# Expert loop of a mixture-of-experts block: order of gate/up and down over the items, shape of the weight chunks, place of the down bias

## The reference

```python
top_vals, top_idx = lax.top_k(logits, 4)
top_w = softmax(top_vals)
# for each expert e, over the tokens that chose it:
gu = xb @ w_gate_up[e] + b_gate_up[e]          # (.., 2048)
gate = minimum(gu[:, :1024], 7.0)
up = clip(gu[:, 1024:], -7.0, 7.0)
hid = (up + 1.0) * gate * sigmoid(1.702 * gate)
y = hid @ w_down[e] + b_down[e]                # (.., 1024)
out[token] += y * top_w
```

## Time and profile before

| | us |
|---|---|
| median of 3 runs | 2227.3 |
| lowest, highest | 2226.61, 2228.27 |
| span of the profiled execution | 2221.8 |
| TensorE busy | 2018.8 (91%) |
| DVE busy | 1551.4 (70%) |
| ACT busy | 1263.3 (57%) |
| GpSimd busy | 513.2 (23%) |

### The profile page before, as it was taken

One profiled execution on the slowest core, in us unless ns is written; L12 is line 12 of the kernel. 1 busy time (PEld: TensorE's weight loads), 2 busy tenths in 40 slices (PEclk: granted clock), 3 DMA queues, 4 the chain that ended last, 5 costly groups with the idle time before them and its releaser, 6 DMA issues. The chain is left out here.

```text
span 2221.8 us, 27993 instructions
## 1 busy us (share of the span) xinstructions
PE 2018.8 (91%) x9545; PEld 1620.9 (73%) x9545; DVE 1551.4 (70%) x1320; ACT 1263.3 (57%) x1173; POOL 513.2 (23%) x396
## 2 busy tenths in 40 slices
PE   7999997888799994999999999999999999999990
PEld 6888886777788874777777777777777777777770
DVE  3433565665423346788888888888888888888885
ACT  4223443333333222777777777777777777777771
POOL 2000005555200002123222222322222223223230
PEclk9999998999899995999999999999999999999995
DMA  4232211120023225899999999999999999999965
GB/s 154 84 106 92 98 38 29 29 67 0 27 88 133 95 79 180 300 344 331 353 334 340 350 329 351 334 337 354 331 345 342 328 359 328 345 345 330 356 233 208
DMA packets 227631, 511.33 MB, mean 230 GB/s; under 512 B 18052, under 2 KB 27396, under 8 KB 226500
## 3 DMA queue, kind: packets, MB, share of 16 engines
q1 hardware_dynamic: 218228, 476.65, 61.5%
q0 software_dynamic: 9360, 34.08, 3.9%
HBM read 484.98 MB, written 20.97 MB: 228 GB/s over the span
## 5 line engine op out<-in xcount | busy, mean ns | idle before, releaser
L1736 DVE TENSOR_TENSOR mlo<-mraw,mhi 128x2048 fp32r<-128x2048 f32 x386 | 909.1, 2382 | 169.1 <-ACT mhi L1685 169.1
L1685 ACT ACTIVATE mhi<-mraw 128x2048 fp32r<-128x2048 f32 x386 | 732.5, 1913 | 174.7 <-PE PM L1816 174.3
L1813 PE MATMUL PM<-mhi,xgT_hi 128*128 128x512 f32 x1024 | 414.4, 405 | 0.0
L1814 PE MATMUL PM<-mlo,xgT_hi 128*128 128x512 f32 x1024 | 407.3, 398 | 0.0
L1816 PE MATMUL PM<-mhi,xgT_lo 128*128 128x512 f32 x1024 | 322.3, 396 | 0.0
L1813 PE MATMUL PM<-mhi,hT_hi 128*128 128x512 f32 x512 | 209.1, 408 | 36.3 <-DVE hT_lo L1761 36.3
L1813 PEld LDWEIGHTS PM<-mhi,xgT_hi 128*128 128x128 f32 x1024 | 193.3, 189 | 65.1 <-issue 23.7
L1663 POOL TENSOR_TENSOR glu<-glu 128x512 f32<-128x512 f32 x64 | 146.5, 2290 | 397.4 <-DVE glu L1755 397.4
L1816 PEld LDWEIGHTS PM<-mhi,xgT_lo 128*128 128x128 f32 x1024 | 192.7, 188 | 46.6
L1814 PEld LDWEIGHTS PM<-mlo,xgT_hi 128*128 128x128 f32 x1024 | 193.1, 189 | 43.4
L1814 PE MATMUL PM<-mlo,hT_hi 128*128 128x512 f32 x512 | 202.4, 395 | 0.0
(11 more groups left out here) (309 smaller groups left out, 3025.2 us busy)
## 6 DMA issues: line engine op xcount, KB each, us to landing
mraw<-in_w_gate_up_dram SPq DMA_DIRECT2D x512, 512.0 KB, 5.2
mraw<-in_w_down_dram SPq DMA_DIRECT2D x256, 512.0 KB, 6.9
raw<-in_w_in_dram SPq DMA_DIRECT2D x28, 1024.0 KB, 5.1
qkvT<-in_w_in_dram SPq DMA_DIRECT2D x8, 1024.0 KB, 5.2
mraw<-expert_rows_scratch SPq DMA_DIRECT2D x8, 1024.0 KB, 11.4
stage<-qkvT SPq DMA_DIRECT2D x3, 1536.0 KB, 7.8
qkvT<-in_w_o_gdn_dram SPq DMA_DIRECT2D x4, 1024.0 KB, 5.1
qkvT<-in_w_o_sconv_dram SPq DMA_DIRECT2D x4, 1024.0 KB, 5.0
```

Source lines behind the costliest of these rows:

```text
L1685: nc.scalar.activation(mhi[:, m % SPL], mraw[:, m % RAW], ACT.Copy).then_inc(e_h, 1)
L1736: nc.vector.tensor_tensor(mlo[:, m % SPL], mraw[:, m % RAW], mhi[:, m % SPL].bitcast(F32), ALU.subtract).then_inc(e_l, 1)
L1813: pe.matmul(PM[:, bank + n, :], t_hi[:, k, :], w_hi[:, kk, n, :], start=False, stop=False)
L1814: pe.matmul(PM[:, bank + n, :], t_hi[:, k, :], w_lo[:, kk, n, :], start=False, stop=False)
```

## The change

The 12 chunks of an item stay 1 MB each, but a gate/up chunk is now 128 whole rows of 2048 columns (8 KB runs, one transfer), and a down chunk is two blocks of 128 whole rows (4 KB runs, one transfer). One gate/up pass goes over all four banks with 8 chunks. The loop's body is now: gate/up of item i + 1 with the turning of item i's hidden rows after its third chunk, then down of item i, with the turning of the tokens of item i + 2 after its first chunk. The first gate/up stands ahead of the loop and the last down behind it. Clamps, sigmoid, gating, the GpSimd product, the splits of hidden and tokens and the y copy handle 1024 columns at once. The hidden and the token rows share banks 6 and 7. `expert`, `pick` and `bias` have 128 rows (the added ones are zero) and `pick` has a column per item. The bias of down is no longer added in the loop: routing builds `mix_w` (token x expert mixing weights), and behind the loop TensorE multiplies it with `b_down`; the last block adds that to `h_rows`. GpSimd's share in splitting the bias and chunk 0 goes to DVE.

The core of the diff (the waits and bodies that only change their index are left out):

```diff
-        EARLY = 1
+        FIRST = 8
...
+        def load_gate_up(sp, e, k, m):
+            one = gu[bass.ds(e, 1), k].rearrange("a p c -> (a p) c")
+            sp.dma_start(mraw[:, raw_slot(m), :], one).then_inc(s_mraw[raw_slot(m)], 16)
...
+        def weights_hi(act, i, m):
+            act.wait_ge(s_mraw[raw_slot(m)], 16 * loads_of_slot(i, m))
+            act.wait_ge(e_used, chunk_number(i, m) + 1)
+            nc.scalar.activation(mhi[:, split_slot(m), :], mraw[:, raw_slot(m), :], ACT.Copy).then_inc(e_h, 1)
...
                 for half in range(2):
                     rows = slice(E * half, E * half + E)
-                    sp.dma_start(bias_raw[rows, 0:2 * D], b_gate_up[0]).then_inc(s_br, 16)
-                    sp.dma_start(bias_raw[rows, 2 * D:3 * D], b_down[0]).then_inc(s_br, 16)
-                for m in range(RAW + EARLY):
-
-                    wait(sp, e_l, m - RAW + 1)
-                    load_weights(sp, 0, m)
+                    sp.dma_start(bias_raw[rows, :], b_gate_up[0]).then_inc(s_br, 16)
+                for k in range(RAW):
+                    load_gate_up(sp, 0, k, 4 + k)
+                sp.dma_start(b_out[:], b_down[0]).then_inc(s_br, 16)
...
-                act.wait_ge(s_br, 64)
-                nc.scalar.activation(bias[:], bias_raw[:], ACT.Copy).then_inc(s_bh, 1)
+                act.sem_inc(e_used, SPL)
+                act.wait_ge(s_br, 48)
+                nc.scalar.activation(bias[0:2 * E, :], bias_raw[:], ACT.Copy).then_inc(s_bh, 1)
+                weights_hi(act, -1, 4)
                 act.wait_ge(s_d4, 1)
                 nc.scalar.activation(ex4, d4, ACT.Exp).then_inc(s_ex4, 1)
+                for m in range(5, 8):
+                    weights_hi(act, -1, m)
...
+                link(nc.vector.tensor_tensor(at_place[:], chosen[:], weight[:].unsqueeze(2).to_broadcast([P, K4, E]), ALU.mult))
+                link(nc.vector.tensor_reduce(mix_w[:], at_place[:].rearrange("p (t k) e -> p t e k", t=TT), AX, ALU.add))
+                for m in range(4, 6):
+                    weights_lo(dve, -1, m)
...
+                with pool.Fori(0, last) as i:
+
+                    pool.wait_ge(s_tx, i + 2)
+                    gather(i + 2)
+                    pool.wait_ge(s_th, i + 1)
+                    hidden(i + 1)
+                    scatter(i)
...
+                with act.Fori(0, last) as i:
+                    for m in range(2, 6):
+                        weights_hi(act, i, m)
+                    hidden_hi(i)
+                    for m in range(6, 12):
+                        weights_hi(act, i, m)
+                    sigmoid(i + 1)
+                    tokens_hi(i + 2)
+
+                    act.wait_ge(e_used, chunk_number(i, 0) + 1 + SPL)
+                    pick_expert(i + 2)
+                    weights_hi(act, i, 12)
+                    weights_hi(act, i, 13)
+                    y_copy(i)
...
+                with dve.Fori(0, last) as i:
+                    for m in range(2, 6):
+                        weights_lo(dve, i, m)
+                    hidden_lo(i)
+                    for m in range(6, 11):
+                        weights_lo(dve, i, m)
+                    clamp(i + 1)
+                    weights_lo(dve, i, 11)
+                    gated(i + 1)
+                    tokens_lo(i + 2)
+                    weights_lo(dve, i, 12)
+                    weights_lo(dve, i, 13)
...
+                with pe.Fori(0, last) as i:
+
+                    pe.wait_ge(s_gate, i + 1)
+                    pe.wait_ge(s_up, i + 1)
+                    gate_up(i + 1, 0)
+                    down(i, 8, between=i + 2)
+                pe.wait_ge(s_gl, last + 2)
+                turn_hidden(last)
+                down(last, 0)
...
                 for t in range(TT):
+                    dve.wait_ge(s_bo, 2 * t + 2)
+                    nc.vector.tensor_tensor(h_rows[:, t, :].rearrange("p (b c) -> p b c", b=2), PM[:, 2 * t:2 * t + 2, :],
+                                            h_rows[:, t, :].rearrange("p (b c) -> p b c", b=2), ALU.add).then_inc(s_hb, 1)
+                dve.wait_ge(s_hb, TT)
```

More of the change, by code:

```diff
@@ L1585, in hybrid_block @@
         xgT_lo = keep("xgT_lo", [P, KD, P], F32R)
-        glu = keep("glu", [P, 2, 4, GW])
+        glu = keep("glu", [P, 4, D])
+        gate, up, sig, hid = (glu[:, n, :] for n in range(4))
         hT_hi = keep("hT_hi", [P, KD, P], F32R)
@@ L1672, in body @@
                     pool.sem_inc(s_yfree, 1)
-                all_items(pool, body)
+                gather(0)
+                pool.wait_ge(s_tx, 1)
+                gather(1)
+                hidden(0)
+                with pool.Fori(0, last) as i:
[4 more added lines that the diff above has]
+                    scatter(i)
+                scatter(last)
+                pool.wait_ge(s_xg, 16 * last + 32)
@@ L1730, in _, with pick_expert, sigmoid @@
-                all_items(act, body)
+                    act.wait_ge(s_tx, i + 1)
+                    nc.scalar.activation(xgT_hi[:], turn_bank, ACT.Copy).then_inc(s_gh, 1)
+                def pick_expert(i):
+                    nc.scalar.activation(expert[:], ones_row[:], ACT.Copy, scale=pick[:, bass.ds(i, 1)]).then_inc(s_exp2, 1)
+                def sigmoid(i):
+                    act.wait_ge(s_gate, i + 1)
+                    nc.scalar.activation(sig, gate, ACT.Sigmoid, scale=ALPHA).then_inc(s_sig, 1)
@@ new lines, in down @@
+                def down(i, m0, between=None):
+                    pe.wait_ge(s_hl, i + 1)
+                    pe.wait_ge(s_y, i + 1)
+                    for d in range(4):
+                        m = m0 + d
+                        pe.wait_ge(e_l, chunk_number(i, m) + 1)
+                        w_hi, w_lo = (w[:, split_slot(m), :].rearrange("p (kk n c) -> p kk n c", kk=2, n=2) for w in (mhi, mlo))
+                        for kk in range(2):
+                            k = 2 * d + kk
+                            for n in range(2):
+                                pe.matmul(y_bank[:, n, :], hT_hi[:, k, :], w_hi[:, kk, n, :], start=(k == 0), stop=False)
+                                pe.matmul(y_bank[:, n, :], hT_hi[:, k, :], w_lo[:, kk, n, :], start=False, stop=False)
+                            for n in range(2):
+                                mm = pe.matmul(y_bank[:, n, :], hT_lo[:, k, :], w_hi[:, kk, n, :], start=False, stop=(k == KD - 1))
+                        mm.then_inc(e_used, 1)
+                        if d == 0 and between is not None:
+                            turn_tokens(between)
```

342 lines of the change are left out of this document (154 added, 188 removed).

## The result

The kernel after takes **2107.6 us** (median of 4 runs, 2103.5 to 2109.4), the kernel before 2227.1 (4 runs): ratio 0.9462, 95% interval 0.9449 to 0.9476. Forecast were 2145 us with a range of 2128 to 2183.

The account below looks back on a forecast made before the run. TensorE's instruction stream was taken as the bound. First bias product at 892.6 + 25.4 + 3.8 + 31 periods (1151.7) + 14.8 = 2088.3; with the tail, span 2139.5, plus 5.5 gives 2145 us, range 2128 to 2183.

Parts of the forecast that it names:

- the period of 37.15 us: TensorE's time per expert-loop item after the change, 2.85 us less than 40.00; bounds 36.8 and 37.7.
- The 144 products stay: 33.6: TensorE's 512-column products of one item, started every 0.233 us, keep their 33.6 us.
- The bias group: Four bias products per item on TensorE instead of three pairs: 1.13 to 1.5 us, taken as 1.3.
- The turning groups: Two groups of eight TensorE transposes per item, each 0.7 to 1.04 us plus 0.11: 2.0 for both.
- The loop's edge: TensorE's loop branch and register work, no longer covered by anything: 0.25 us per item (0.1 to 0.6).
- What could be late next: Loop check of split copies, DVE, gather chain and weight loads against TensorE's needs: all in time, loads costed at nothing.
- X: The end of an item's last down product on TensorE, from which the forecast counts times.
- the DVE rival: DVE, delayed by GpSimd's port use, bounds the loop: period 38.3 us, time 2181 us; chance 13%.
- the chain's: In the loop, GpSimd's scatter and gather bring tokens late: example period 43.1 us, time 2330 us; chance 10%.
- no stall was kept: Rival: loop edge or transposes cost more, stalls remain; period 38.5 to 39.5 us, time 2187 to 2218; chance 8%.
- The DMA rival: Weight transfers bound the loop: period 38.4 us, time 2184 us (2174 by the skill's limit); chance 9%.
- The mix products: Eight bias products behind the loop: 7.5 us, ending before the last scatter lands, up to 3 us more otherwise.

Follow-up runs that it names:

- the last experiment: Kernel after with 2880 unused bytes, plus earlier b_out load and exponential, mix weights turned in routing, two mix products in the hT_lo wait: 2088.6 us, ratio 0.9381.
- +2880 bytes: Kernel after with 2880 unused bytes ahead of the tile `expert`, so xgT and hT match mhi and mlo modulo 4096: 2099.4 us.
- after +1152: Kernel after with 1152 unused bytes ahead of its small tiles, so xgT_hi and hT_hi stand modulo 4096 where they stood before: 2128.3 us.
- after +2944: Kernel after with 2944 unused bytes ahead of `expert`: 2127.4 us.
- before +2944: Kernel before with 2944 unused bytes, putting xgT_hi and hT_hi at exactly the bytes of the kernel after: 2211.9 us, ratio 0.9945.
- after +3392: Kernel after with 3392 unused bytes ahead of `expert`: 2099.2 us.

## Why the prediction was too high

Worked out by its own steps, spans against spans:

| step | forecast | measured | difference |
|---|---|---|---|
| first bias product | 892.6 | 899.2 | +6.6 |
| first gate/up | 25.4 | 25.8 | +0.4 |
| uncovered turning | 3.8 | 3.75 | 0 |
| 31 periods | 1151.7 | 1108.0 | -43.7 |
| last item | 14.8 | 14.7 | -0.1 |
| from the last product to the end | 51.2 | 54.1 | +2.9 |
| median less span | 5.5 | 2.0 | -3.5 |

The sum is 2145 - 37.4 = 2107.6. The 31 periods are 30 of 35.69 and a first one of 37.36: behind a wait of 2.70 us at 928.79 the granted clock is 0.55 from 928.9 to 932.3 and the products there start 0.43 apart; the forecast had no term for it. The last row is the profiled execution: where the record has time and span of one execution they stand 1.7 to 2.3 apart (2107.66 and 2105.6 here, 2221.58 and 2219.6 for the kernel before), so the forecast's 5.5 held some 3.5 us by which the profiled execution of before was faster than its median. The late start and the longer end, 9.5 us, hide a part of the miss: by luck the time lies nearer to the forecast than the periods do.

**The step that failed is the period of 37.15 us** with its bounds of 36.8 and 37.7; 35.69 was measured. Its mechanism was right: the waits for hT_lo and for the expert row are gone, nothing else came late. Four sizes in it were not, all on the same side, and the largest is the term that was taken over unchanged:

- "The 144 products stay: 33.6." They stay in number, but came every 229.3 ns instead of 233.3: 33.0, 0.59 less, 18 us of the 44. This term had been given no bounds at all. With the low end of each other term (1.13, twice 0.81, 0.1) the sum is 36.45, 0.76 above what was measured, and 0.59 of that is this term. The experiments show the cause, the place in SBUF: with the place of before the kernel after takes 2128.3 us, the low end of the range; the other three terms make the rest.
- The bias group, 1.3 (1.13 to 1.5), is 0.93. The earlier trace rows show entry and exit for 64 rows; I kept them for 128, and the runs with 64 and 128 rows show that they go (0.39 in the kernel after): 0.37 less, 11.5 us.
- The turning groups, 2.0, are 1.76: 7.4 us. The 0.7 to 1.04 of the text was the length of a group; what counts is the distance between starts, 0.80 and 0.08.
- The loop's edge, 0.25 (0.1 to 0.6), is not seen: the last two products of an item and the bias group behind them start 0.23 apart each (1500.99 to 1501.45). TensorE's branch and register work do not show: 7.8 us.

So where do the 4.31 us an item come from? Stalls 1.13 + 0.80; bias products 2.55 to 0.93, that is 1.62; transposes 1.93 to 1.76, 0.17; the products' spacing 0.59. Together 4.31. Less than half is what the pipelining itself took away. Of the bias's 1.62, the 128 rows are some 0.75 (kernel before: 0.59 in the period and 0.16 in the longer wait) and the down pair then 0.48 (measured in the kernel after); the other 0.4, two pairs made one group behind no wait, was not run by itself. The prediction's signs of being wrong looked for a period above 37.7 only, none below; its other sign, a first bias product after 896, did come (899.2), by the loop's start below.

**What could be late next** was worked out well. Lo of chunk 2 at X + 5.3 (forecast 5.5), DVE 33.9 (35.9 had been given, with GpSimd's product taking 2.6 from it; the row below shows 2.41 for the whole and 5.86 instead of 4.48 for the subtractions next to it, so 1.4 was taken), tokens landed at X + 20.7 (12.4 to the gather's issue, 8.3 to its landing; forecast 21.6) and wanted at X + 26.6.

```profile
1503.99 1.03 POOL L1692 DMA_INDIRECT expert_rows_scratch<-y_rows,now  x1 [0.17 <-issue]
...
1513.87 1.01 POOL L1679 DMA_INDIRECT xg<-xn_scratch,now  x1
...
1532.69 2.41 POOL L1685 TENSOR_TENSOR glu<-glu 128x1024 f32<-128x1024 f32 x1 [17.82 <-DVE glu L1791]
```

So neither the DVE rival nor the chain's came, and no stall was kept. The DMA rival fell with 383 GB/s in the period. The Trainium skill (DMA: Bandwidth & Descriptors, "Where 436 GB/s comes from") has about 358 GB/s between HBM and SBUF; an estimate from that figure puts the period at 38.1 us at least. This case does not agree: 383 GB/s, with one core at work. The share was no sign of a full queue either: it is 0.96 at 341 and at 383 GB/s.

**The loop's start** is 6.6 us late. The rows, ACT, DVE, GpSimd and TensorE in turn:

```profile
869.34 1.91 ACT L1512 ACTIVATE bias<-bias_raw 64x2048 fp32r<-64x2048 f32 x1 [26.04 <-DMA b_out<-in_b_down_dram]
...
873.06 1.28 ACT L1515 ACT_TABLE_LOAD   x1
...
874.60 0.17 DVE L1570 TENSOR_REDUCE small<-small 128x4 f32<-128x16 f32 x1 [6.13 <-ACT small L1515]
...
887.44 1.26 POOL L1679 DMA_INDIRECT xg<-xn_scratch,now  x1 [0.38 <-issue]
...
894.87 1.97 PE L1827 MATMUL PM<-ident,xg 128*128 128x128 f32 x8 [25.85 <-DMA xg<-xn_scratch,now]
```

The wait for the exponential was foreseen, in the right place, at 871; it ended at 874.6. Of these 3.6 us 1.5 had come from the stages before (routing began at 848.0 instead of 846.6) and 2.1 from b_out, which landed at 869.3 and not 866. The other 3.0 are the gather: 7.4 us from issue to tokens, where the forecast kept the 4.4 of before; in the last experiment it took 8.8. SP asks for the next weight chunks at 886.35, 1.1 us ahead of it, and the DMA engines move 418 GB/s at a share of 0.99 from 890 to 892, while in the kernel before SP asked 3.8 us after the gather's issue (884.20 and 880.36). That may be what holds it up; no run took them away.

**The mix products** were priced at 7.5 us and took 11.6:

```profile
2051.46 0.60 PE L1888 MATMUL PM<-ident,mix_w 128*32 128x128 f32 x4
2053.20 11.64 PE L1894 MATMUL PM<-b_out,mix_wT 32*128 32x512 f32 x16 [1.14 <-ACT mix_wT L1769]
```

The windows view from there on (granted clock third from the right):

```profile
2053.00:2055.00 2.00, 1.80 (x4) 0.85 (x5) 0.00 (x0) 0.15 (x1) 0.99 (x1) 1.00 0.18 74
2055.00:2057.00 2.00, 2.00 (x5) 0.74 (x4) 0.00 (x0) 0.00 (x0) 0.00 (x0) 0.66 0.47 188
2057.00:2059.00 2.00, 2.00 (x4) 0.95 (x3) 0.00 (x0) 0.00 (x0) 0.00 (x0) 0.50 0.00 0
```

The price was right at the clock of the loop: in the last experiment six of them follow the down products with no gap, at granted clock 1.00 from 2039 to 2042 and 0.90 from there, and take 0.94 each; eight would be 7.5. In the kernel after, TensorE waits 1.14 us for mix_wT, works 2 to 3 us at granted clock 1.00 and is at 0.50, the lower of its two levels (1.2 of 2.4 GHz), for the rest. Whether the pause brings the clock down was not tried by itself, and the waits alone do not sort the cases: behind the last item's wait for hT_lo the clock stays at 1.00 here (2.57 us, to 2040.35), and with +2880 bytes it is at 0.54 from 2032.3 to 2035.6 (2.69 us, to 2031.38). The last experiment's block ends 9.3 us after the scatter's issue; by that the scatter of the kernel after is through at 2062.4 and the products, which end at 2064.8, outlast it by 2.4 us, the case for which the text had kept "up to 3 us".

## What to carry to other kernels

Where TensorE is the bound, the distance between the starts of its products is a quantity of its own: average it over the whole loop, before and after, and give it bounds in a forecast, since tiles that only change size ahead of its operands can move it by 3%. Read an edit's cost off distances between starts, and ask whether the row from which it is taken has the same shape: entry and exit of 64-row products don't hold for 128 rows. And when a change frees TensorE, ask how much of it an existing wait takes back: 0.15 us of 0.6 to 0.75 in the kernel before, nothing in the kernel after, whose loop has no such wait. And look at the block ahead of the loop for the small load that is queued last and waited for first, and at the one behind it for small products that run after a pause.

## What was not expected of the hardware

In these kernels the place of the operands in SBUF sets how often a 128x128x512 product starts, by up to 3%. Remainders by 256 of the byte at which the stationary tile stands, with that of the moving tiles at 224 throughout:

| xgT_hi, remainder by 256 | kernels | ns between starts |
|---|---|---|
| 32 | before; after +1152; after +2944 | 233.3, 233.4, 233.4 |
| 160 | after; before +2944 | 229.3, 229.2 |
| 224 | after +2880; after +3392 | 227.1, 227.1 |

Seven kernels with five different addresses by 4096 fall into three values, and 64 bytes (+2880 to +2944) change the time by 28 us, with 512 bytes (+2880 to +3392) doing nothing. The mixer's products, whose operands, moving and stationary, all stand at remainder 224, come every 226.7 ns in every one of these kernels. Whether the distance between the two operands counts or the stationary tile's own place was not told apart (the moving tiles stayed where they were), and no other remainder (96, say) was tried. Nor did any run show the mechanism; that the rows of the bias, the runs of the transfers and the products' order have no part in it the runs with each of them show, and that the other engines have none, the windows in which they stand still.
